# Gathered expert tiles: four rows for each of 32 tokens instead of one row for each of 128

## What is computed

```python
def peer(h, w_query, sub_keys, expert_u, expert_v):
    q = (h @ w_query).reshape(B, S, PEER_HEADS, 2, PEER_HALF)
    sc = jnp.einsum('bshcd,hckd->bshck', q, sub_keys)
    sv, si = lax.top_k(sc, PEER_TOPK)
    cand_s = (sv[..., 0, :, None] + sv[..., 1, None, :]).reshape(...)
    cand_i = (si[..., 0, :, None] * N_KEYS + si[..., 1, None, :]).reshape(...)
    top_s, top_j = lax.top_k(cand_s, PEER_TOPK)
    eidx = jnp.take_along_axis(cand_i, top_j, axis=-1)
    gate = jax.nn.softmax(top_s, axis=-1)
    ...
    u, v = expert_u[et], expert_v[et]          # 128 experts for each token
    act = jax.nn.gelu(jnp.einsum('tnd,td->tn', u, xt)) * gt
    return jnp.einsum('tn,tnd->td', act, v)
```

## Time and profile before

| | |
|---|---|
| median of 3 runs | 1682.56 us |
| the profiled execution | 1685.36 us, of which the span 1683.8 us |
| TensorE busy | 1394.0 us (83%), mean granted clock 0.922 |
| VectorE busy | 1029.3 us (61%) |
| ScalarE busy | 358.7 us (21%) |
| GpSimd busy | 347.3 us (21%) |
| DMA | 407 MB, 297 of it on the gathers' queue |

### The profile page before, as it was taken

How to read it: one execution, slowest core, us unless ns; L and a number is a source line. 1 busy time by engine, 2 the same in 40 slices (tenths; PEclk the granted TensorE clock), 3 DMA queues, 4 the chain that set the end, 5 groups by cost and what they waited for, 6 DMA issues and landing times.

```text
span 1683.8 us, 24922 instructions
## 1 busy us (share of the span) xinstructions
PE 1394.0 (83%) x10614; PEld 940.2 (56%) x10614; DVE 1029.3 (61%) x2175; ACT 358.7 (21%) x696; POOL 347.3 (21%) x315
## 2 busy tenths in 40 slices
PE   7989898957677797588859897779987878899997
PEld 6468764832233264255525554347877763788843
DVE  2967765539999877868788777421554343355511
ACT  3012400112222322421242121212342210111100
POOL 1000011124344444445545454000000000000000
PEclk9988998979887898899988998789999999899998
DMA  9453387599989999799999999524200021344442
GB/s 373 165 176 116 110 323 259 187 324 420 373 323 383 366 356 407 267 391 416 419 376 365 418 417 415 219 75 150 101 8 3 4 103 50 112 151 154 154 159 83
DMA packets 110735, 406.98 MB, mean 242 GB/s; under 512 B 10376, under 2 KB 35472, under 8 KB 77344
## 3 DMA queue, kind: packets, MB, share of 16 engines
q0 software_dynamic: 44576, 297.35, 44.3%
q1 hardware_dynamic: 62720, 104.36, 18.1%
q10 hardware_dynamic: 3328, 3.68, 1.2%
HBM read 404.30 MB, written 1.07 MB: 241 GB/s over the span
## 4 chain that ended last, share of the span: by engine, by line
PE 58%; DVE 23%; DMA 8%; ACT 5%; issue 4%; POOL 1%; ACTq 0%; DVEq 0%; another core or an unknown queue 0%
PE psum L489 24%; DVE arena L1197 9%; PE psum L499 7%; PE psum L1231 6%; PE psum L1582 6%; DMA arena<-in_experts,arena 6%; PE psum L2038 4%; PE psum L1785 2%; DMA weights<-in_w_in 1%; PE psum L585 1%; DVE arena L1156 1%; DVE arena L1157 1%; DVE arena L1154 1%; PE psum L708 1%; PE psum L1926 1%
## 5 line engine op out<-in xcount | busy, mean ns | idle before, releaser
L1231 PE MATMUL psum<-arena 128*128 128x512 f32 x792 | 405.9, 665 | 142.0 <-ACT arena L1219 141.6
L489 PE MATMUL psum<-actT,weights 128*128 128x256 f32 x1824 | 404.0, 384 | 5.3 <-ACT actT L602 2.3
L1187 POOL DMA_INDIRECT arena<-in_experts,arena x256 | 317.5, 1240 | 437.9 <-PE psum L1231 370.5
L489 PEld LDWEIGHTS psum<-actT,weights 128*128 128x128 f32 x1824 | 351.1, 193 | 57.5 <-ACT actT L602 5.6
L1231 PEld LDWEIGHTS psum<-arena 128*128 128x128 f32 x792 | 161.8, 212 | 348.7 <-issue 200.3
L1197 DVE CUSTOM_DVE_ANT_0 arena<-normed,arena 128x1024 f32<-128x1024 f32 x256 | 304.7, 1223 | 61.1 <-DMA arena<-in_experts,arena 57.0
L1213 ACT ACTIVATE arena<-arena 128x3 f32<-128x3 f32 (+1 forms) x86 | 17.6, 204 | 441.0 <-DVE arena L1197 384.2
L1582 PE MATMUL psum<-arena 64*64 64x64 f32 (+1 forms) x2816 | 84.6, 224 | 17.5 <-DVE arena L1699 7.1
L1582 PEld LDWEIGHTS psum<-arena 64*64 64x64 f32 x2816 | 79.3, 135 | 24.5 <-issue 14.9
L499 PE MATMUL psum<-weights,actT 128*128 128x512 f32 x192 | 83.1, 593 | 2.1 <-DMA weights<-in_w_in 1.0
L944 POOL DMA_DIRECT2D arena<-in_ada_wT x48 | 25.3, 528 | 252.0 <-DVE mod L960 252.0
(11 more groups left out here) (347 smaller groups left out, 1537.4 us busy)
## 6 DMA issues: line engine op xcount, KB each, us to landing
weights<-in_w_in SPq DMA_DIRECT2D x18, 2048.0 KB, 8.9
arena<-in_ada_wT POOLq DMA_DIRECT2D x48, 512.0 KB, 5.8
weights<-in_ffn_w_up SPq DMA_DIRECT2D x22, 1024.0 KB, 6.8
weights<-in_ffn_w_down SPq DMA_DIRECT2D x5, 2048.0 KB, 7.9
weights<-in_w_out SPq DMA_DIRECT2D x4, 2048.0 KB, 15.0
weights<-in_w_peer_q SPq DMA_DIRECT2D x4, 2048.0 KB, 8.5
arena<-in_experts,arena POOLq DMA_INDIRECT x256
weights<-in_w_ple_gate SPq DMA_DIRECT2D x2, 2048.0 KB, 8.2
```

Source lines behind the costliest of these rows:

```text
L489: mm = nc.tensor.matmul(out[:, c * T:(c + 1) * T], w[:, k, c * P:(c + 1) * P], act[:, k, :], start=(k == 0), stop=(k == kc - 1))
L1187: nc.gpsimd.indirect_dma_start(out=rows[:, n % RING, :], out_offset=None, in_=dram["experts"], in_offset=bass.IndirectOffsetOnAxis(ap=eidx ...
L1231: mm = nc.tensor.matmul(SUMS[:, i, :], diag[:, pos, :], rows[:, pos, D + 512 * i:D + 512 * (i + 1)], start=first, stop=last, skip_group_ch ...
```

## The change

Each gather now brings four rows for each of 32 tokens: gather k of a block serves the tokens of quarter k%4, and partition 32j + t holds row 4*(k//4) + j of token t of that quarter. Index and gate matrices have to stand in that layout. VectorE spreads each selection's result over four column groups, masked by `quad`; TensorE brings it to the right partitions by four small matmuls with `ident_q` (`pe_spread`); VectorE copies it from PSUM. The tokens have to stand four times, once in each 32 partitions: `normed` is written to DRAM (`normed_rows`) and read back by four DMAs for each half into `quad_tokens`, for block 0 ahead of the gathers, for block 1 behind its last groups.

The sum of a row tile has a stationary operand of 128x32 instead of 128x128 and writes one quarter of the PSUM partitions. A group has two gathers, of neighbouring quarters; in `pe_group` the matmuls of the two stand next to each other for each half of the columns. `row_used` is counted in the second half. All 256 tiles go this way: L1208, the waits for `row_added` and the wide groups are gone. The product with the gate (L1201) moves to ScalarE, one activation a number, so VectorE no longer waits for gelu within a group. The ring has 8 slots, and the space of the ninth holds the second half of the tokens.

There are now 128 turns. A selection has ten pieces, one a turn, and a new selection starts every 8 turns, so the seven end with turn 57; the pieces behind them are the same, one a turn, and end with turn 118. `pe_ctx_in` and `dve_scan_common` get waits for what stands ahead in PSUM.

```diff
-RING = 9
-GROUP = 3
+RING = 8
+GROUP = 2
+QUADS, QP = 4, 32
...
+    put("ident_q", np.eye(QP)[i % QP])
+    put("quad", (i[:, None] // QP) == np.arange(QUADS)[None])
...
-        diag = r.take(RING * P).rearrange("p (g n) -> p g n", g=RING)
+        dots, gelu, acts = [r.take(RING).rearrange("p (g n) -> p g n", n=GROUP) for _ in range(3)]
+        diag = r.take(RING * QP).rearrange("p (g n) -> p g n", g=RING)
         rows = r.take(RING * 2 * D).rearrange("p (g n) -> p g n", g=RING)
+        high = r.take(2 * D).rearrange("p (g n) -> p g n", g=2)
+        quad_tokens = (normed, high)
...
-        SELECT_PIECES = 5
+        SELECT_PIECES = 10
+        SELECT_EVERY = 8
+        SPREAD = {what: PS[:, 2 * (tile_at["ctx_k"] % 2) + i, 0:HEADS * PK] for i, what in enumerate("eg")}
+        FIRST_E = AUX[:, 0, 0:HEADS * PK]
+        def pe_spread(pe, what, turn, dst):
+            pe.wait_ge(S(f"spread_{what}_in"), turn + 1)
+            if turn:
+                pe.wait_ge(S("eidx_ok" if what == "e" else "gates_done"), turn)
+            src = spread_e if what == "e" else spread_g
+            n = HEADS * PK
+            for j in range(QUADS):
+                mm = nc.tensor.matmul(dst[QP * j:QP * (j + 1), :], K("ident_q"), src[:, n * j:n * (j + 1)],
+                                      start=True, stop=True)
+            mm.then_inc(S(f"spread_{what}"), 1)
+        def pe_select(pe, b, quarter):
+            for _ in range(SELECT_PIECES - 1):
+                yield
+            for what in "eg":
+                pe_spread(pe, what, QUARTERS * b + quarter, SPREAD[what])
+            yield
+        def act_quad_tokens(act, b, half):
+            for j in range(QUADS):
+                src = normed_rows[b * P:(b + 1) * P].rearrange("(g t) d -> t g d", g=QUADS)
+                act.dma_start(quad_tokens[half][QP * j:QP * (j + 1), :, :], src[:, 2 * half:2 * half + 2, :]).then_inc(
+                    S(f"quad_in{half}"), 16)
...
+                if i == QUARTERS - 1:
+                    pe_spread(pe, "e", 0, FIRST_E)
...
+                    if i == QUARTERS - 1:
+                        pe_spread(pe, "g", 0, SPREAD["g"])
+                        pe.wait_ge(S("eidx_ok"), 1)
...
+            act.wait_ge(S("normed_ok"), so_far("n2", TB, TB))
+            act.dma_start(normed_rows.rearrange("(b p) d -> p b d", p=P), normed).then_inc(S("normed_out"), 16)
...
+                if i == 1:
+                    act.wait_ge(S("normed_out"), 16)
+                    act.wait_ge(S("turn_pe"), so_far("n2", DC // 2, DC // 2))
+                    for half in range(2):
+                        act_quad_tokens(act, 0, half)
...
+            st.link(nc.vector.tensor_copy(gsum, tsc[:, :, 0]))
+            nc.vector.tensor_tensor(tsc, tsc, bc(gsum, P, n_h, PK), ALU.subtract).then_inc(S("gate_sub"), 1)
             for h in range(n_h):
+                if h:
+                    yield
...
-            nc.vector.tensor_copy(eidx[:, b, es], eif).then_inc(S("eidx_ok"), 1)
-            st.link(nc.vector.tensor_copy(gsum, tsc[:, :, 0]))
-            nc.vector.tensor_tensor(tsc, tsc, bc(gsum, P, n_h, PK), ALU.subtract).then_inc(
-                S("gate_sub"), 1)
+            n = n_h * PK
+            quad = K("quad").unsqueeze(1).to_broadcast([P, n, QUADS])
+            nc.vector.tensor_tensor(spread_e.rearrange("p (n g) -> p n g", g=QUADS), bc(eif, P, n, QUADS), quad,
+                                    ALU.mult).then_inc(S("spread_e_in"), 1)
+            if turn == 0:
+                dve.wait_ge(S("spread_e"), 1)
+                nc.vector.tensor_copy(eidx[:, b, es], FIRST_E).then_inc(S("eidx_ok"), 1)
+            yield
             dve.wait_ge(S("gate_exp"), turn + 1)
             st.link(nc.vector.tensor_reduce(gsum, tsc, AX_X, ALU.add))
             st.link(nc.vector.reciprocal(gsum, gsum))
-            nc.vector.tensor_tensor(gate[:, b, es].rearrange("p (h k) -> p h k", h=n_h), tsc,
-                                    bc(gsum, P, n_h, PK), ALU.mult).then_inc(S("gates_done"), 1)
+            st.link(nc.vector.tensor_tensor(tsc, tsc, bc(gsum, P, n_h, PK), ALU.mult))
+            nc.vector.tensor_tensor(spread_g.rearrange("p (n g) -> p n g", g=QUADS),
+                                    bc(tsc.rearrange("p h k -> p (h k)"), P, n, QUADS), quad,
+                                    ALU.mult).then_inc(S("spread_g_in"), 1)
+            yield
+            yield
+            if turn:
+                dve.wait_ge(S("spread_e"), turn + 1)
+                nc.vector.tensor_copy(eidx[:, b, es], SPREAD["e"]).then_inc(S("eidx_ok"), 1)
+            dve.wait_ge(S("spread_g"), turn + 1)
+            nc.vector.tensor_copy(gate[:, b, es], SPREAD["g"]).then_inc(S("gates_done"), 1)
             dve.wait_ge(S("gates_done"), turn + 1)
             yield
...
                     g, j = divmod(k, GROUP)
-                    if j == ON_PE and not wide(former[0], t, g):
-                        pool.wait_ge(S("row_added"), dve_added(former[0], t, g) + 1)
-                    else:
-                        pool.wait_ge(S("row_used"), pe_summed(former[0], t, g) + j + 1)
+                    pool.wait_ge(S("row_used"), rows_ahead(former[0], t, g) + j + 1)
...
         def dve_group(dve, b, t, g, count):
+            half = g % 2
+            if isinstance(t, int) and t == 0 and g < 2:
+                dve.wait_ge(S(f"quad_in{half}"), 16 * QUADS * (b + 1))
             for k, pos, n, filled in turn_slots(b, t, g * GROUP, count):
                 dve.wait_ge(S(f"row{pos}"), filled * 16)
                 j = k - g * GROUP
-                ins = nc.vector.tensor_tensor_reduce(rows[:, pos, 0:D], normed[:, b, :], rows[:, pos, 0:D], 1.0, 0.0,
+                ins = nc.vector.tensor_tensor_reduce(rows[:, pos, 0:D], quad_tokens[half][:, j, :], rows[:, pos, 0:D], 1.0, 0.0,
                                                      ALU.mult, ALU.add, dots[:, g, j:j + 1])
             ins.then_inc(S("dots_ok"), 1)
-            dve.wait_ge(S("gelu_ok"), t * PER_TURN + (GROUPS * b + g + 1))
-            nc.vector.tensor_tensor(acts[:, g, 0:count], gelu[:, g, 0:count],
-                                    gate[:, b, bass.ds(t * RING + g * GROUP, count)], ALU.mult).then_inc(S("acts_ok"), 1)
-            if count == GROUP and not wide(b, t, g):
-                dve.wait_ge(S("acts_ok"), t * PER_TURN + (GROUPS * b + g + 1))
-                added = dve_added(b, t, g)
-                if not isinstance(added, int) or added > 0:
-                    dve.wait_ge(S("row_added"), added)
-                nc.vector.scalar_tensor_tensor(xres[:, b, :], rows[:, pos, D:2 * D], acts[:, g, ON_PE:GROUP],
-                                               xres[:, b, :], ALU.mult, ALU.add).then_inc(S("row_added"), 1)
         def act_group(act, b, t, g, count):
             act.wait_ge(S("dots_ok"), t * PER_TURN + (GROUPS * b + g + 1))
             nc.scalar.activation(gelu[:, g, 0:count], dots[:, g, 0:count], ACT.Gelu_apprx_tanh).then_inc(S("gelu_ok"), 1)
-            act.wait_ge(S("acts_ok"), t * PER_TURN + (GROUPS * b + g + 1))
+            if isinstance(t, int):
+                act.wait_ge(S("gates_done"), QUARTERS * b + (t * RING + g * GROUP + count - 1) // (NSEL // QUARTERS) + 1)
+            act.wait_ge(S("gelu_ok"), t * PER_TURN + (GROUPS * b + g + 1))
+            for j in range(count):
+                nc.scalar.activation(acts[:, g, j:j + 1], gelu[:, g, j:j + 1], ACT.Copy,
+                                     scale=gate[:, b, bass.ds(t * RING + (g * GROUP + j), 1)]).then_inc(S("acts_ok"), 1)
             for k, pos, n, filled in turn_slots(b, t, g * GROUP, count):
                 j = k - g * GROUP
-                if j < ON_PE or wide(b, t, g):
-                    nc.scalar.activation(diag[:, pos, :], K("ident"), ACT.Copy,
-                                         scale=acts[:, g, j:j + 1]).then_inc(S("diag_ok"), 1)
+                act.wait_ge(S("acts_ok"), rows_ahead(b, t, g) + j + 1)
+                nc.scalar.activation(diag[:, pos, :], K("ident_q"), ACT.Copy,
+                                     scale=acts[:, g, j:j + 1]).then_inc(S("diag_ok"), 1)
+            if b + 1 < TB and isinstance(t, int) and t == TURNS - 1 and g >= PER_TURN - 2:
+                act_quad_tokens(act, b + 1, g % 2)
         def pe_group(pe, b, t, g, count):
-            for k, pos, n, filled in turn_slots(b, t, g * GROUP, count):
-                j = k - g * GROUP
-                if j == ON_PE and not wide(b, t, g):
-                    continue
-                pe.wait_ge(S("diag_ok"), pe_summed(b, t, g) + j + 1)
-                first = isinstance(t, int) and t == 0 and k == 0
-                last = isinstance(t, int) and t == TURNS and k == REST - 1
-                for i in range(2):
-                    mm = nc.tensor.matmul(SUMS[:, i, :], diag[:, pos, :], rows[:, pos, D + 512 * i:D + 512 * (i + 1)],
+            pe.wait_ge(S("diag_ok"), rows_ahead(b, t, g) + count)
+            for i in range(2):
```

(15 more changed lines are left out.)

## The result

The changed kernel takes 1702.8 us (median of four runs, 1700.9 to 1705.9) where the kernel before takes 1682.5 (1682.3 to 1685.5). The ratio is 1.0118 with an interval of 1.0099 to 1.0137: slower by 20 us, where 1645 us were forecast. The profiled execution took 1703.4 us, with a span of 1701.8.

The account below looks back on a forecast made before the run. Gathers at 419 GB/s were the floor, with engines holding them back in most windows. Lost transfer time 39.5 us where 68 stood, end -11.6, start +1: about -40, so 1645 us; own range 1630 to 1662, wider range 1616 to 1680.

Parts of the forecast that it names:

- selections (372 to 680): Selection stage: transfers become the bound with VectorE 91% full; 4 us of transfer time lost where 27 stood.
- context products, first direction, second block's tokens: Middle of the stage: 13 us lost in products and first direction where 23 stood, plus 3 for block 1's tokens.
- second direction: Start of the second direction: 32 us for 10 gathers, 25 us, less ring cover; 5 us lost, 8 before.
- scan windows: The two long scan windows: a turn takes 4.55 us against 5.0 of transfers; 6 us charged for both, 10 before.
- `ple_proj` ahead of the last turns: Turn 118 of 128: TensorE waits for loads and works 8.80 us while the ring holds eight gathers; 6 us charged.
- The tokens of block 1: Block 1's token loads: 2 MB more, 5 us of transfer, partly hidden in the context products; 3 us charged.
- Each of its 7 turns loses ... 2.9 us of VectorE, so 61.9 - 20 = 42 us for 14 gathers, 35 us: 7 over: Start of the first direction: dot product, L1208 and wait removed from each turn, leaving 7 us over the transfers.
- A full ring covers some 6 of these 19: Context products (12 us over) and first direction (7 over): the ring hides some 6, so 13 lost where 23 stood.
- loads or waits keep a turn at 5.5 us: Rival on scan-window turns: unhidden weight loads or cross-engine waits add 21 us, giving 1666; chance 0.16.
- The end: Behind the last landing: 5.6 us where 17.2 stood, 11.6 gained; ple_proj's stop before it charged at 6 us.
- quarters that don't run together: Rival on TensorE's sums: a scan-window turn takes 6.35 us for two gathers, +52 us, giving 1697; chance 0.12.

Follow-up runs that it names:

- e6_same_quarter: Changed kernel with both rows of a group summed into the same quarter of PSUM's partitions (sums at wrong tokens): 1754.9 us, ratio 1.0413.
- e1_no_tokens: Changed kernel without the eight loads of the second block's tokens and VectorE's wait for them: 1688.7 us, ratio 1.0037.
- e2_packed_lora: Changed kernel with the last context product's 512 KB of weights laid out in DRAM as 4 KB in a row per partition: 1693.2 us, ratio 1.0046.
- e12_no_tokens_packed: Changed kernel with the edits of e1_no_tokens and e2_packed_lora together: 1688.3 us, ratio 1.0023.
- e7_spaced: Changed kernel with light turns moved beside the heavy scan and direction pieces and ple_proj at the last turns: 1686.3 us, ratio 1.0011.
- e8_dve_lag2: Changed kernel with VectorE's piece one turn later in its own order, behind the dot products of two turns on: 1702.2 us, ratio 1.0104.
- e16_every8: e13_end with a selection every 8 turns again and no light turns between the context products: 1646.7 us, ratio 0.9779.
- e3_late_ple: Changed kernel with ple_proj's two pieces 7 turns later, at the last turns: 1693.3 us, ratio 1.0050.
- e13_end: Edits of e7_spaced, e2_packed_lora and e8_dve_lag2, selections every 7 turns, light turns between products, ple_proj's matmuls behind the last row sums: 1647.7 us, ratio 0.9789.

## Why the prediction was wrong

In the prediction's own terms, with the transfer time lost against 419 GB/s from the windows after:

| term | predicted, us | measured, us |
|---|---|---|
| selections (372 to 680) | 4 | 4.8 + 0.5 |
| context products, first direction, second block's tokens | 13 + 3 | 19.0 + 20.1, and 5.0 for the 2.1 MB |
| second direction | 5 | 11.0 |
| scan windows | 6 | 5.7 + 7.3 |
| `ple_proj` ahead of the last turns | 6 | 5.0 + 3.0, and 12.5 for other loads ahead of the last gathers |

The measured side is 57 us above the predicted one; 1099.1 less 1043 is 56. Windows cut by hand can't tell 1 us, so that closeness is in part chance.

**Right.** VectorE's additions and products with the gate are gone and the selections are held by the transfers: 412 GB/s, forecast "near 410", with VectorE 83% busy where some 90% were forecast. A turn's sums take 1.91 us (forecast 1.9), and e6_same_quarter shows that it is the quarters that do it. The context products take 7.2 us a turn (7.1). The rule of the Trainium skill that was weighed (TensorE: Matmul & The Clock Gate, "The mechanism"), that a weight load overlaps matmuls only on another row group, is not what the trace shows: all rows are in use, and a group's eight loads lie inside its unbroken 1.91 us of matmuls (the group at 714.98 above):

```profile
714.98 0.14 PEld L1274 LDWEIGHTS psum<-arena 128*32 128x32 f32 x4 [1.17 <-ACT arena L1262]
715.44 0.12 PEld L1274 LDWEIGHTS psum<-arena 128*32 128x32 f32 x2 [0.31 <-issue]
715.87 0.12 PEld L1274 LDWEIGHTS psum<-arena 128*32 128x32 f32 x2 [0.31 <-issue]
```

In e6_same_quarter they do so on a single quarter too, one about every 0.43 us. The same section also lets a load into a background weight buffer go ahead, which the prediction left out; no run tells whether that is the case here. Behind the gathers nothing changed, 602 us both times.

**The tokens of block 1** ("5 us of transfer, in part in the context products, where transfers have room ... 3 us") is the first step that failed. They did fit in beside the products. But they drained the ring at the moment at which the last 512 KB of context weights were asked for. A small-packet load beside a full gather queue gets 26 GB/s, and TensorE stood 9.7 us; the turn took 12.6 more than its 7.2. e1_no_tokens, e2_packed_lora and e12_no_tokens_packed each take 10 to 15 us away, and both edits together no more than one. The prediction looked at the bytes of the added load and not at what stood behind them in time.

**"Each of its 7 turns loses ... 2.9 us of VectorE, so 61.9 - 20 = 42 us for 14 gathers, 35 us: 7 over"** failed twice. The count was wrong: the stretch has six turns, not seven (from 651.34 to 713.17 in the kernel before, by the starts of their dot products, 61.8 us). With six the same subtraction gives 44.4 us for 12 gathers, 30 us: 14 over. And the subtraction of busy time was wrong: the six turns take 51.0 us after the change (737.29 to 788.26), 21 over. Two of them did lose the whole 2.90 us (7.57 became 4.67, 6.33 became 3.43). The other four lost 1.07 to 1.84, since VectorE stands idle in them, mostly for another engine, and that idle time got longer by nearly all that VectorE no longer does. In the turn shown above VectorE waits 5.61 us for ScalarE's piece; before:

```profile
676.35 2.29 DVE L1517 TENSOR_TENSOR_SCAN arena<-const,weights 128x1024 f32<-128x1024 f32 x1 [3.78 <-ACT arena L1485]
```

The wait grew by 1.83 and the turn shrank by 1.07 (13.87 to 12.80), together 2.90. The second direction repeats it: five turns take 37.3 us, 12 over, where 5 were charged. With light turns (e7_spaced) both directions transfer faster. e8_dve_lag2 raises them too, but by itself it gives no time that is clear of the noise.

**"A full ring covers some 6 of these 19"** was too hopeful. The turns of the two directions are 21 and 12 us over, and the transfers lost 20.7 and 12.0: the ring covered nothing that can be seen. The heavy pieces stand in a row, with no light turn between them that would empty a ring full of landed rows. Light turns among the direction's pieces give 7 us; light turns among the products, with the denser selections that make room for them, give nothing (e16_every8).

**The scan windows** were mis-sized, 6 for 13. 4.55 us a turn was TensorE's busy time. By the waits it is a chain that sets the pace, from TensorE to VectorE and ScalarE and back, with stops of 0.4 us in it, which a turn of three gathers seems to have covered. No run tests this. This is the rival "loads or waits keep a turn at 5.5 us" in part: 5.2 to 5.3 was measured.

**The end** ("I charge 6", and 5.6 us behind the last landing) had the stall and the tail about right: transfers end near 1092 and the sums are read at 1099. It left out what else moves with `ple_proj`: the gate's weights and rows, 5.24 MB, came before the last gathers instead of behind them. e3_late_ple gave 9 us back and e13_end, with TensorE's own part moved as well, about 10 more.

None of the named rivals came true as a whole. The price of the one with the wrong premise, quarters that don't run together, was +52 us, and 1754.9 less 1702.8 is 52; its main part, the scan windows, was right, and two other parts that did not come happen to cancel. The slower side got 0.14 for two mechanisms. What made the kernel slower was a sum of four places, each of which the forecast had charged at half or less. e13_end comes to 1647.7 us, against a forecast of 1645, with the added loads and moved pieces where they disturb less. That it comes so close is in part chance: it has several edits that the forecast did not count on, and some of its gain may be the chip's.

## What to carry to other kernels

When a transfer-bound stage gets more bytes or a moved piece, list every load that is asked for in the same stretch, the size of its packets, and who waits for it; a load that used to find the queue idle may now share it packet by packet. A turn's new length is the longest chain through all engines in that turn, read off the timeline, and not the old length less the removed busy time; and the turns of a stretch are counted there too. If a piece with its own weights is moved, the loads behind it in the same queue move with it.

## What the runs showed of the hardware

- Two DMA queues that both have work share packet by packet: 773 and 771 packets in 15 us, 8 KB beside 512 bytes. 512 KB of 512-byte packets took 30 us beside the gathers, and came within one stretch of 5 us where 152 of the gathers' packets passed beside them (e1_no_tokens).
- Eight loads into 32 partitions each, beside the gathers, brought both together down to 277 GB/s from 419. Neither the source rows nor packets of twice the size changed that (277 and 249 GB/s). The cause is open.
- A load whose source repeats the same rows four times in its outermost dimension ran on about four of the 16 engines: 93 GB/s nearly alone.
- Two quarters of TensorE's columns run together at full row use, 1.91 us for four matmuls of 512 columns against 3.62 on one quarter, with their weight loads inside that time, and they need not be neighbours in the order.
- TensorE stops for about 0.4 us 16 to 33 times in 250 us of dense 64x64 matmuls, with no releaser in the profile, in every profile but the four of one chip (none to 6 there). Shifting its program by 64 instructions changed nothing.
